# A hybrid transformer's mixing stage: projection jobs placed on both sides of each attention unit's transposes

## The chip, the cores and the metric

The kernel runs on one core of one Trainium2 chip. The metric is the device time of one execution in microseconds; lower is better. TensorE (PE) multiplies, VectorE (DVE) and ScalarE (ACT) work beside it, SyncE (SP) issues the DMAs, and GpSimd (POOL) has nothing to do in the part that is changed. Each engine runs its own instructions in program order, and semaphores join them.

## The reference

The computed function is a one-layer block (retention and RWKV mixing, then a mixture of experts) followed by a two-layer block, for 256 tokens of width 1024, all in float32. The change lies in the two layers of the second block, which are, for each layer:

```python
h = rmsnorm(x, norm_mix[layer])
z = h @ w_in[layer]                       # 18 groups of columns
o_a = nsa_mixer(...)      # compressed, selected and window attention, 4 heads
o_b = diff_mixer(...)     # difference of two softmaxes, 4 heads of 2 halves
o_c = mlstm_mixer(...)    # convolution, gated linear recurrence, 4 heads
o_d = dilated_mixer(...)  # attention over dilated key sets, 4 heads
x = x + concatenate([o_a, o_b, o_c, o_d], axis=-1) @ w_out[layer]
h = rmsnorm(x, norm_ffn[layer])
x = x + (silu(h @ w_gate[layer]) * (h @ w_up[layer])) @ w_down[layer]
```

## The kernel before

`mixing(nc, K, layer)` (L2025) builds one layer's stage from the norm to the product with `w_out`; it is called twice. It holds one instruction stream for each engine: `tensor` (PE), `scalar` (ACT), `vector` (DVE) and `sync` (SP). The order of the work in each is written out by hand in the same lists.

**Jobs.** The projection `h @ w_in` is cut into 22 jobs, `j0` to `j21`. Each is 8 matrix products over the 8 blocks of 128 input features, which the trace shows as 16 matmul records. The jobs `j0`, `j1`, `j14` and `j15` are 512 columns wide (`L2161`), `j20` and `j21` are 256 wide at `L2161`, and the other 16 write 128 feature rows for 256 tokens (`L2158`). ACT copies each result from PSUM to SBUF (`L2342`).

**Other items.** `bq`, `bk`, `aq`, `ks`, `dq` and `dk` are rotations (rotary embedding): one product with a swap matrix on PE (`L2177`, 2 records), then three DVE operations (`rotate`, `L2439`, `L2441`, `L2443`), the last of which counts up `rotated`. `cmp` makes the compressed keys and values (`L2182`, `L2185`), `mq0`, `mq1`, `qk0` and `qk1` belong to the mLSTM, `f` sums its forget gates, and `o0` to `o3` transpose outputs for the last product.

**Banks.** Items take the PSUM banks 6 and 7 in turn (`qk0` and `qk1` take both). PE waits ahead of an item until ACT or DVE has taken the earlier item out of its bank (`held`, `ordinal`).

**Units.** The attention work is 14 units: 0 to 3 are "diff", 4 and 5 "cmp", 6 and 7 "slc", 8 and 9 "win", 10 and 11 "mlstm", 12 and 13 "dil". A unit goes round all three engines:

- `score(u)` on PE (`L2231` for diff, `L2254`, `L2238`) makes the scores in banks 0 and 1, once the scores before have been taken (`scores_kept`).
- `maxima(u)` on DVE (`L2460` masks and moves them, `L2471` takes the row maxima).
- `exps(u)` on ACT (`L2365` and `L2363`).
- `weigh(u)` on DVE (`L2490` to `L2494` for diff, `L2508` for others) normalises and counts up `p_ready`.
- `turn(u)` on PE (`L2268`, `L2264`) transposes the probabilities; it waits for `p_ready`.
- `keep(u)` on ACT (`L2383`, `L2377`) copies them to SBUF.
- `values(u)` on PE (`L2289`, `L2282`) multiplies them with the values, and `output(u)` on DVE takes the result.

**Order on PE.** First the items of `before_units`, then `score(0)`, and then for each unit u: `score(u + 1)`, `turn(u)`, the items of `fills[u]`, `values(u)`. All filling jobs of a unit stand behind its transposes. `score(0)` follows `j7`, which follows `bk`.

**Order on ACT.** The copies of all `before_units`, then the exponentials for `lambdas` and `forget_gates` (`L2407`, `L2409`, with the load of the table for Exp ahead of them), `exps(0)`, and for each unit `keep(u)`, `exps(u + 1)`, the copies of `fills[u]`. Behind those of unit 4 stands a block of other functions (`L2419` to `L2424`), with three table loads.

**Order on DVE.** `lambdas()`, `rotate("bq")`, `rotate("bk")`, `forget_gates()`, a wait for ACT's exponentials (`lam_exp`) with two small operations (`L2595`, `L2596`), `maxima(0)`, and for each unit `weigh(u)`, `maxima(u + 1)`, `output(u - 1)`, then `convolve()` (`L2553`, `L2556`) in unit 0, `cut_blocks()` (`L2569`, behind the copy of `j11`) in unit 1, and the rotations of `fills[u]`.

The weights come as 2 MB slots of a ring of five (`WeightStream`), loaded as PE starts on a later slot. `K.both` shares semaphores between the two layers.

Of the kernel before, what the change touches and what calls it, by code (L numbers as in the profile page):

```python
# [15 lines left out]
KT = D // P  # L16
# [2008 lines left out]
def mixing(nc, K, layer):  # L2025
# [19 lines left out]
    f, fa = A.temp(TT, 4), A.temp(TT, 4)  # L2045
# [26 lines left out]
    before_units = ["j0", "j1", "j2", "j3", "j4", "bq", "j5", "j6", "bk", "j7"]  # L2072
    fills = [["j8", "j9"], ["j10", "j11"], ["j12", "j13", "cmp"], ["aq", "j14"], ["ks", "j15"], ["j16", "mq0"], ["j17", "mq1"],
             ["j18", "f"], ["j19", "dq"], ["j20", "dk", "qk0"], ["j21", "qk1"], ["o0"], [], []]
    after_units = ["o3", "o1", "o2"]
    (x_in, x_at), place_free = K.x_ready, K.place_free
    items = before_units + [name for fill in fills for name in fill] + after_units
    at = {name: n for n, name in enumerate(items)}
    by = lambda name: "dve" if name in turns or name in ("f", "qk0", "qk1") else "act"
    ordinal = [sum(by(other) == by(name) for other in items[:n + 1]) for n, name in enumerate(items)]  # L2080
    banks, held, turn_of = [], [], {6: -1, 7: -1}
# [49 lines left out]
    def tensor(pe):  # L2131
# [13 lines left out]
        def job(n, bank):  # L2145
# [5 lines left out]
            for k in range(KT):  # L2151
# [14 lines left out]

        def item(name):
            n = at[name]
            for m in held[n]:
                pe.wait_ge(took[by(items[m])], ordinal[m])  # L2170
            bank = banks[n][0]
            if name[0] == "j":
                last = job(int(name[1:]), bank)
# [123 lines left out]
        score(0)  # L2297
        for u in range(NU):
            if u + 1 < NU:
                score(u + 1)  # L2300
            turn(u)
            for name in fills[u]:
                item(name)
            values(u)
# [28 lines left out]
    def scalar(act):  # L2333
# [70 lines left out]
        for name in before_units:  # L2404
            item(name)
# [3 lines left out]
        nc.scalar.activation(fa, fa, ACT.Exp, scale=-1.0).then_inc(f_exp, 1)  # L2409
        exps(0)  # L2410
        for u in range(NU):
            keep(u)
            if u + 1 < NU:
                exps(u + 1)
            for name in fills[u]:
                item(name)
# [13 lines left out]
    def vector(dve, meanwhile):  # L2430
# [160 lines left out]
        rotate("bq")  # L2591
        rotate("bk")
# [3 lines left out]
        link(nc.vector.tensor_scalar(nlam, nlam, -lam_init, None, ALU.add))  # L2596
        maxima(0)
        for u in range(NU):
# [5 lines left out]
            if u == 0:  # L2604
                convolve()
            if u == 1:
                cut_blocks()
            for name in fills[u]:
# [661 lines left out]
```

## Time and profile before

| what | us |
|---|---|
| median of 3 runs | 2032.84 |
| lowest and highest of them | 2032.58, 2036.86 |
| the profiled execution's own time | 2041.22 |
| its span in the trace | 2039.3 |
| PE busy (matmuls) | 1699.0 |
| DVE busy | 699.8 |
| ACT busy | 358.4 |

The two mixing stages lie at about 1166 to 1376 us (layer 0) and 1599 to 1810 us (layer 1) of the span; a feed-forward stage follows each. In the timeline a line merges the neighbouring instructions of one source line; the length is from the first start to the last end, and since matmuls are pipelined the next line may start a little before that. The number in brackets is the idle time of the engine just before the line. "PEclk" in the windows is the granted clock of TensorE as a share of its full speed; its two levels are 0.50 (1.2 GHz) and 1.00 (2.4 GHz), and a window in between holds a change.

### The profile page before, as it was taken

The page shows a single profiled execution, that of the slowest core. Times are in us where ns is not written, and L with a number is a line of the kernel's source. Part 1 is how long each engine was busy: PE and PEld are TensorE (multiplying, and loading weights), DVE is VectorE, ACT ScalarE, POOL GpSimd, SP SyncE. Part 2 cuts the span into 40 slices and gives each one's busy share as a digit, 9 for nine tenths or more (in the row PEclk, how much of TensorE's full clock was granted, in tenths as well). Part 3 has the DMA queues.
Part 4 walks back from the last instruction along what each step waited for, and adds up shares of the span by engine and source line. Part 5 has one row for each costly group of instructions (what it writes and reads, how often), then busy time and mean ns, then how long its engine had stood idle before and what let it go on. Part 6 is the DMA issues. An engine that isn't in the chain of part 4 may idle for free.

```text
span 2039.3 us, 31978 instructions
## 1 busy us (share of the span) xinstructions
PE 1699.0 (83%) x14184; PEld 1161.0 (57%) x14184; DVE 699.8 (34%) x1247; ACT 358.4 (18%) x827; POOL 90.9 (4%) x94
## 2 busy tenths in 40 slices
PE   6999889988989675565465589989999989899997
PEld 3665458957975531221121266749994566669963
DVE  2005372353332300000000133554663243546663
ACT  2010212332231210000000222421000124310000
POOL 0000004302311000000000000000000000000000
PEclk9999898977999787877787889989999989899999
DMA  9421110040024599999999932214454522125440
GB/s 372 193 100 67 66 50 36 4 166 2 4 88 153 212 430 427 428 428 428 427 427 428 421 107 83 83 47 182 174 184 161 216 83 83 68 98 191 173 184 21
DMA packets 35593, 382.08 MB, mean 187 GB/s; under 512 B 6977, under 2 KB 10433, under 8 KB 12673
## 3 DMA queue, kind: packets, MB, share of 16 engines
q1 hardware_dynamic: 35458, 380.04, 46.5%
q8 instruction: 113, 1.85, 0.4%
q14 instruction: 22, 0.18, 0.0%
HBM read 378.98 MB, written 1.05 MB: 186 GB/s over the span
## 4 chain that ended last, share of the span: by engine, by line
PE 48%; DMA 11%; DVE 4%; ACT 2%; issue 1%; SPq 0%; DVEq 0%; ACTq 0%
PE psum L2722 14%; PE psum L1873 7%; PE psum L2793 7%; DMA arena<-in_w_moe 6%; PE psum L2158 6%; DMA weight_ring<-in_w_moe 5%; PE psum L2161 3%; PE psum L2313 3%; PE psum L1848 3%; PE psum L2289 1%; PE psum L2268 1%; PE psum L1828 1%; PE psum L2177 1%; ACT arena L2365 0%; PE psum L2254 0%
## 5 line engine op out<-in xcount | busy, mean ns | idle before, releaser
L1873 PE MATMUL psum<-weight_ring,arena 128*32 128x512 f32 x640 | 142.3, 721 | 127.8 <-DMA arena<-in_w_moe 93.7
L1269 PE MATMUL psum<-arena 64*64 64x64 f32 x4608 | 152.4, 224 | 20.5 <-PEq L962 9.1
L2722 PE MATMUL psum<-arena 128*128 128x128 f32 x1408 | 165.2, 275 | 1.7 <-DVE arena L2925 1.7
L2722 PEld LDWEIGHTS psum<-arena 128*128 128x128 f32 x1408 | 161.1, 192 | 2.0 <-issue 2.0
L1269 PEld LDWEIGHTS psum<-arena 64*64 64x64 f32 x4608 | 144.7, 139 | 28.0 <-issue 23.9
L1873 PEld LDWEIGHTS psum<-weight_ring,arena 128*32 128x32 f32 x640 | 35.9, 129 | 205.5 <-issue 205.5
L2002 DVE COPY arena<-psum 128x512 f32<-128x512 f32 x16 | 11.1, 692 | 371.1 <-PE psum L1873 371.1
L2722 PE MATMUL psum<-arena,weight_ring 128*128 128x128 f32 x1056 | 131.9, 283 | 4.7 <-ACT arena L2839 2.7
L1873 PE MATMUL psum<-arena 128*32 128x512 f32 x384 | 106.8, 716 | 33.6 <-DMA weight_ring<-in_w_moe 33.1
L2722 PEld LDWEIGHTS psum<-arena,weight_ring 128*128 128x128 f32 x1056 | 127.3, 199 | 5.9 <-DVE arena L2970 3.1
L2158 PE MATMUL psum<-arena,weight_ring 128*128 128x256 f32 x512 | 123.8, 401 | 0.0
L2158 PEld LDWEIGHTS psum<-arena,weight_ring 128*128 128x128 f32 x512 | 103.0, 204 | 18.7 <-ACT arena L2342 1.8
L2908 DVE TENSOR_TENSOR arena<-weight_ring 128x1024 f32<-128x1024 f32 (+1 forms) x72 | 81.3, 1129 | 55.4 <-PE psum L2793 55.2
L1453 DVE TENSOR_TENSOR arena<-arena,psum 128x512 f32<-128x512 f32 (+1 forms) x80 | 50.6, 633 | 88.1 <-PE psum L1269 87.3
L2793 PE MATMUL psum<-arena 128*128 128x512 f32 x176 | 78.5, 592 | 0.0
L2161 PE MATMUL psum<-weight_ring,arena 128*128 128x512 f32 (+1 forms) x192 | 76.2, 552 | 2.6 <-DVE arena L2582 1.3
L2793 PE MATMUL psum<-weight_ring,arena 128*128 128x512 f32 x132 | 63.3, 620 | 9.7 <-DVE arena L2908 6.0
L434 PE MATMUL psum<-arena,weight_ring 128*128 128x256 f32 x288 | 65.7, 391 | 2.8 <-PEq L198 2.8
L1923 ACT ACTIVATE arena<-psum 128x256 f32<-128x256 f32 x16 | 6.2, 386 | 348.0 <-PE psum L1883 348.0
L434 PEld LDWEIGHTS psum<-arena,weight_ring 128*128 128x128 f32 x288 | 56.4, 197 | 11.4 <-issue 3.3
L1848 PE MATMUL psum<-arena 128*128 128x512 f32 x128 | 59.3, 605 | 1.2 <-ACT arena L1938 1.2
L2313 PE MATMUL psum<-weight_ring,arena 128*128 128x512 f32 x128 | 59.4, 624 | 0.0
(497 smaller groups left out, 2252.4 us busy)
## 6 DMA issues: line engine op xcount, KB each, us to landing
weight_ring<-in_w_moe SPq DMA_DIRECT2D x60, 2048.0 KB, 20.2
arena<-in_w_moe SPq DMA_DIRECT2D x36, 2048.0 KB, 20.5
weight_ring<-in_w_in SPq DMA_DIRECT2D x23, 2048.0 KB, 8.4
weight_ring<-in_w_mod SPq DMA_DIRECT2D x12, 2048.0 KB, 8.1
weight_ring<-in_w_gate SPq DMA_DIRECT2D x12, 2048.0 KB, 7.7
weight_ring<-in_w_up SPq DMA_DIRECT2D x12, 2048.0 KB, 7.6
weight_ring<-in_w_down SPq DMA_DIRECT2D x12, 2048.0 KB, 7.6
weight_ring<-in_w_out SPq DMA_DIRECT2D x6, 2048.0 KB, 7.8
```

The source lines that it names most:

```text
L434: last = nc.tensor.matmul(bank[:, 0:T], w[:, k, P * b:P * b + P], hT[:, k, T:2 * T], start=(k == 0), stop=(k == KT - 1))
L1269: last = nc.tensor.matmul(K.ps[half[d], bank, column + HD * n:column + HD * n + HD], lhs(d, h), rhs(d, h), start=True, stop=True, skip_gro ...
L1453: done = nc.vector.tensor_tensor(inv[:, par, 0:kinds, which, :], inv[:, par, 0:kinds, which, :], src, ALU.add)
L1828: last = nc.tensor.matmul(K.ps[:, d % 4, 0:256], K.h2[:, t, P * d:P * d + P], sel[:, t, cols], start=(t == 0), stop=(t == 1))
L1848: last = nc.tensor.matmul(K.ps[:, 2 * t + n, :], scatter_to[:, e, P * t:P * t + P], parts[:, n, :], start=(e == 0), stop=(e == NE - 1))
L1873: last = nc.tensor.matmul(K.ps[strip(j), 4, :], xsT[:, k, CAP * e:CAP * e + CAP], ws[j][:, k, :], start=(k == 0), stop=(k == KT - 1), skip ...
L2158: last = nc.tensor.matmul(K.ps[:, bank, 0:T], w[:, k, P * b:P * b + P], hT[:, k, :], start=(k == 0), stop=(k == KT - 1))
L2161: last = nc.tensor.matmul(K.ps[:, bank, 0:width], hT[:, k, P * b:P * b + P], w[:, k, 0:width], start=(k == 0), stop=(k == KT - 1))
L2313: last = nc.tensor.matmul(K.ps[:, 2 * t + n, :], K.mixT[:, k, P * t:P * t + P], ws[n][:, k, :], start=(g == 0 and k == 0), stop=(g == 2 an ...
L2722: last = nc.tensor.matmul(K.ps[:, bank, P * n:P * n + P], lhs, rhs, start=(n == 0 and k == 0 and name in ("m1", "m5", "m6")), stop=(k == 3 ...
L2793: return nc.tensor.matmul(K.ps[:, int(name[1]) - 1, :], lhs, rhs, start=(j == 0), stop=(j == NFT // 2 - 1), skip_group_check=True)
L2908: nc.vector.tensor_tensor(out, x, y, op).then_inc(sums_ready, 1)
```

## The change

The orders of the three engines in `mixing` are changed, in both layers. No product, copy or vector operation is added or dropped; seven jobs are issued in two halves of 8 records each.

- `j7` leaves `before_units`. On PE it now stands behind `score(0)`, so `score(0)` follows `bk` at once. On ACT its copy stands behind `exps(0)`.
- For the units 0 to 3 one job (`leads`: `j8`, `j10`, `j12`, `j14`) stands on PE between `score(u + 1)` and `turn(u)`, and its copy on ACT ahead of `keep(u)`. The other items stay behind the transposes.
- For the units 4 to 10 one job (`halved`: `j15` to `j21`) is split: four of its eight blocks ahead of `turn(u)`, four behind. Its copy on ACT stands behind `exps(u + 1)`.
- In unit 3 `aq` is now behind `j14`, and in unit 4 `ks` behind `j15`; before, they stood ahead of these jobs.
- The exponentials of `lam` and the forget gates move on ACT from behind all of `before_units` to behind `j1`.
- On DVE `forget_gates()`, the wait for `lam_exp` and the two operations behind it move ahead of `rotate("bq")`, and `convolve()` moves from unit 0 to unit 3. `cut_blocks()` stays in unit 1.

```diff
--- before.py
+++ after.py
@@ -2069,12 +2069,16 @@
     units = [("diff", t, i) for t in range(TT) for i in range(2)]
     units += [(kind, t, 0) for kind in ("cmp", "slc", "win", "mlstm", "dil") for t in range(TT)]
     NU = len(units)
-    before_units = ["j0", "j1", "j2", "j3", "j4", "bq", "j5", "j6", "bk", "j7"]
-    fills = [["j8", "j9"], ["j10", "j11"], ["j12", "j13", "cmp"], ["aq", "j14"], ["ks", "j15"], ["j16", "mq0"], ["j17", "mq1"],
-             ["j18", "f"], ["j19", "dq"], ["j20", "dk", "qk0"], ["j21", "qk1"], ["o0"], [], []]
+    before_units = ["j0", "j1", "j2", "j3", "j4", "bq", "j5", "j6", "bk"]
+    first_fill = "j7"
+    leads = {0: "j8", 1: "j10", 2: "j12", 3: "j14"}
+    halved = {4: "j15", 5: "j16", 6: "j17", 7: "j18", 8: "j19", 9: "j20", 10: "j21"}
+    fills = [["j9"], ["j11"], ["j13", "cmp"], ["aq"], ["ks"], ["mq0"], ["mq1"], ["f"], ["dq"], ["dk", "qk0"], ["qk1"], ["o0"],
+             [], []]
+    around = lambda u: [leads[u]] if u in leads else [halved[u]] if u in halved else []
     after_units = ["o3", "o1", "o2"]
     (x_in, x_at), place_free = K.x_ready, K.place_free
-    items = before_units + [name for fill in fills for name in fill] + after_units
+    items = before_units + [first_fill] + [name for u, fill in enumerate(fills) for name in around(u) + fill] + after_units
     at = {name: n for n, name in enumerate(items)}
     by = lambda name: "dve" if name in turns or name in ("f", "qk0", "qk1") else "act"
     ordinal = [sum(by(other) == by(name) for other in items[:n + 1]) for n, name in enumerate(items)]
@@ -2142,13 +2146,13 @@
                     last = nc.tensor.transpose(K.ps[:, 4 - 2 * place + q, P * k:P * k + P], h[:, t, c:c + P], K.ident)
                 last.then_inc(t_made, 1)
 
-        def job(n, bank):
+        def job(n, bank, ks):
             s, kind, b, width, dst = jobs[n]
             first = s != slot[0]
             if first:
                 slot[0], slot[1] = s, W.take(pe)
             w = slot[1]
-            for k in range(KT):
+            for k in ks:
                 if n == 0 and k == 4:
                     turn_input(1, 0)
                 if n == 1 and k == 0:
@@ -2164,13 +2168,23 @@
                     last.then_inc(W.used, 1)
             return last
 
+        def await_bank(name):
+            for m in held[at[name]]:
+                pe.wait_ge(took[by(items[m])], ordinal[m])
+
+        def half_job(name, i):
+            if i == 0:
+                await_bank(name)
+            last = job(int(name[1:]), banks[at[name]][0], range(4 * i, 4 * i + 4))
+            if i == 1:
+                last.then_inc(made, 1)
+
         def item(name):
             n = at[name]
-            for m in held[n]:
-                pe.wait_ge(took[by(items[m])], ordinal[m])
+            await_bank(name)
             bank = banks[n][0]
             if name[0] == "j":
-                last = job(int(name[1:]), bank)
+                last = job(int(name[1:]), bank, range(KT))
             elif name in turns:
                 pe.wait_ge(rope_landed, 16 * len(rope_in))
                 kept({"bq": "j3", "bk": "j5", "aq": "j9", "ks": "j13", "dq": "j17", "dk": "j19"}[name])
@@ -2295,10 +2309,17 @@
         for name in before_units:
             item(name)
         score(0)
+        item(first_fill)
         for u in range(NU):
             if u + 1 < NU:
                 score(u + 1)
+            if u in leads:
+                item(leads[u])
+            if u in halved:
+                half_job(halved[u], 0)
             turn(u)
+            if u in halved:
+                half_job(halved[u], 1)
             for name in fills[u]:
                 item(name)
             values(u)
@@ -2401,17 +2422,24 @@
         keep_turned(0, 1)
         norm(1, 0)
         keep_turned(1, 0)
-        for name in before_units:
+        for name in before_units[:2]:
             item(name)
         act.wait_ge(lam_ready, once)
         nc.scalar.activation(lsum, lsum, ACT.Exp).then_inc(lam_exp, 1)
         act.wait_ge(f_abs, once)
         nc.scalar.activation(fa, fa, ACT.Exp, scale=-1.0).then_inc(f_exp, 1)
+        for name in before_units[2:]:
+            item(name)
         exps(0)
+        item(first_fill)
         for u in range(NU):
+            if u in leads:
+                item(leads[u])
             keep(u)
             if u + 1 < NU:
                 exps(u + 1)
+            if u in halved:
+                item(halved[u])
             for name in fills[u]:
                 item(name)
             if u == 4:
@@ -2588,12 +2616,12 @@
         scale_turned(1, 0)
         dve.wait_ge(rest_landed, 16 * len(rest_in))
         lambdas()
-        rotate("bq")
-        rotate("bk")
         forget_gates()
         dve.wait_ge(lam_exp, once)
         link(nc.vector.tensor_tensor(nlam, lsum[:, 1:2], lsum[:, 0:1], ALU.subtract))
         link(nc.vector.tensor_scalar(nlam, nlam, -lam_init, None, ALU.add))
+        rotate("bq")
+        rotate("bk")
         maxima(0)
         for u in range(NU):
             weigh(u)
@@ -2601,10 +2629,10 @@
                 maxima(u + 1)
             if u:
                 output(u - 1)
-            if u == 0:
-                convolve()
             if u == 1:
                 cut_blocks()
+            if u == 3:
+                convolve()
             for name in fills[u]:
                 if name in turns:
                     rotate(name)
```

## Rows read from the trace of the kernel before

**Rows 1.** Head of the page: the span, then busy time by engine.

```profile
span 2039.3 us, 31978 instructions
...
PE 1699.0 (83%) x14184; PEld 1161.0 (57%) x14184; DVE 699.8 (34%) x1247; ACT 358.4 (18%) x827; POOL 90.9 (4%) x94
```

**Rows 2.** Waits of PE, 1638.38 to 1755.32 us: who waited for whom, total, times, longest.

```profile
PE psum L2268 <- DVE arena L2494: 6.8, 2, 3.7
```

**Rows 3.** Timeline of PE, layer 1: start, length, line, tiles, count, [idle before, releaser].

```profile
1599.24 1.09 PE L2142 MATMUL psum<-arena 128*128 128x128 f32 x8 [2.14 <-DVE arena L2578]
...
1637.52 1.02 PE L2177 MATMUL psum<-arena 128*128 128x512 f32 x2
1638.38 3.63 PE L2158 MATMUL psum<-arena,weight_ring 128*128 128x256 f32 x16
1641.94 0.71 PE L2231 MATMUL psum<-arena 32*128 32x128 f32 x8
1645.18 1.18 PE L2231 MATMUL psum<-arena 32*128 32x128 f32 x8 [2.53 <-DVE arena L2460]
1649.49 0.69 PE L2268 MATMUL psum<-arena 128*128 128x128 f32 x2 [3.13 <-DVE arena L2494]
1649.97 9.82 PE L2158 MATMUL psum<-arena,weight_ring 128*128 128x256 f32 x32
...
1661.46 7.10 PE L2158 MATMUL psum<-arena,weight_ring 128*128 128x256 f32 x32
```

**Rows 4.** The same timeline, around the transposes of the third unit.

```profile
1673.69 1.12 PE L2268 MATMUL psum<-arena 128*128 128x128 f32 x4 [3.68 <-DVE arena L2494]
1674.60 9.46 PE L2158 MATMUL psum<-arena,weight_ring 128*128 128x256 f32 x32
```

**Rows 5.** Windows on PE, layer 1: length, busy (instructions), granted clock, DMA.

```profile
1600.00:1602.00 2.00, 0.72 (x5) 0.72 0.97 410
1644.00:1646.00 2.00, 0.82 (x8) 0.82 0.00 0
1654.00:1656.00 2.00, 2.00 (x8) 0.62 0.00 0
1672.00:1674.00 2.00, 0.31 (x2) 0.64 0.00 0
1684.00:1764.00 80.00, 74.55 (x513) 1.00 0.22 80
1768.00:1770.00 2.00, 0.49 (x3) 0.53 0.00 0
1780.00:1782.00 2.00, 2.00 (x4) 0.55 0.71 164
```

**Rows 6.** Timeline of DVE, layer 1, same columns as Rows 3.

```profile
1639.90 0.69 DVE L2443 TENSOR_TENSOR arena<-arena 128x512 f32<-128x512 f32 x1
...
1644.05 0.16 DVE L2595 TENSOR_TENSOR arena<-arena 128x1 f32<-128x1 f32 x1 [2.67 <-ACT arena L2407]
...
1644.43 0.69 DVE L2460 SCALAR_TENSOR_TENSOR arena<-psum,arena 128x512 f32<-128x512 f32 x1
...
1669.08 2.25 DVE L2569 TENSOR_TENSOR arena<-arena 64x240 f32<-64x240 f32 x4 [5.10 <-ACT arena L2342]
```

**Rows 7.** Timeline of PE, layer 1, the later units.

```profile
1714.29 1.10 PE L2282 MATMUL psum<-arena 15*128 15x64 f32 x8
...
1717.54 0.66 PE L2268 MATMUL psum<-arena 128*128 128x128 f32 x4 [1.08 <-DVE arena L2508]
...
1739.49 1.09 PE L2268 MATMUL psum<-arena 128*128 128x128 f32 x8 [0.48 <-DVE arena L2508]
...
1755.32 1.14 PE L2207 MATMUL psum<-arena 64*128 64x256 f32 x8 [1.19 <-ACT arena L2342]
```

**Rows 8.** Timeline of PE, layer 0: the same stretch's first and last lines.

```profile
1205.66 3.63 PE L2158 MATMUL psum<-arena,weight_ring 128*128 128x256 f32 x16
...
1322.03 1.14 PE L2207 MATMUL psum<-arena 64*128 64x256 f32 x8 [1.19 <-ACT arena L2342]
```

## The prediction

> **What bounds the kernel now.** I read the head of the page first [rows 1]: PE has a matmul in flight for 1699 of 2039.3 us, and DVE and ACT are below half of that. A change that adds and drops no operation can then only win where PE stands still or runs at its low clock inside the two changed stages. So the second view was the waits of PE from the start of `j7` to the start of `qk1` [rows 2], which names DVE and ACT as releasers and no DMA. The third was PE's timeline of the same stretch [rows 3, 4, 7], where each wait has its place. The fourth was the granted clock there [rows 5], and the last DVE's timeline [rows 6], to see what holds the releasers up. The stretch takes 116.94 us in layer 1 (1638.38 to 1755.32) and 116.37 us in layer 0 (1205.66 to 1322.03) [rows 3, 7, 8], and the two look alike line for line. So I cost layer 1 and count it twice.
>
> Two places lose most. **At the start of the units** PE goes from `score(0)` to `score(1)` over 2.53 us of idle time and from there to `turn(0)` over 3.13 us [rows 3]. The reader is to see why in [rows 6]: DVE is done with `bk` at 1640.59 (1639.90 and 0.69) but stands for 2.67 us until ACT has worked off `j7`'s copy, a table load and two exponentials, and takes up the scores only at 1644.43. From there the round over maxima, exponentials and `weigh(0)` takes 5.06 us to `turn(0)` at 1649.49, and nothing fills it. **At the third unit** `turn(2)` waits 3.68 us [rows 4]; in the DVE timeline `cut_blocks()` waits for the copy of `j11`, runs 2.25 us, and `weigh(2)` stands behind it [rows 6]. Later there are 1.08 us (`turn(6)`) and 0.48 us (`turn(10)`) [rows 7].
>
> Each of the two big waits also costs clock. The granted clock is 0.82 in the window 1644 to 1646, so it falls to 0.50 there, and is 0.62 in 1654 to 1656, so it is back only then; it falls again within 1672 to 1674 [rows 5]. The two jobs behind the first take 9.82 us where two undisturbed ones take 7.10 (16 records follow each other in 3.47) [rows 3]; those behind the second take 9.46 [rows 4].
>
> **The change part by part.** All for one stage.
>
> *`j7` behind `score(0)`, ACT's exponentials and DVE's small work ahead.* DVE will come from `rotate("bk")` straight to `maxima(0)`. The 2.67 us on DVE goes; its cover is the time ahead of `bq`, in which DVE has nothing to do but wait for PE. The ACT step that moves is a table load and two short exponentials, between the copies of `j1` and `j2`, which lie 3.5 us apart; if that were late, `j4` would wait for its bank, a few tenths. The round of 5.06 us starts about 0.8 us after `score(0)` starts. Between that start and `turn(0)` PE now has `score(0)` and `score(1)` (0.64 us each by the pace of the 0.71 us row) and `j7` and `j8` (3.47 each), 8.2 us against 5.9. So both waits go: 2.53 + 3.13 = 5.66 us. With them goes the low clock: 9.82 - 7.10 = 2.72 us on the jobs, 1.18 - 0.71 = 0.47 on `score(1)` and about 0.2 on `turn(0)`. That is 9.0 us.
>
> *The new wait for `bk`.* What is late next is the rotation itself. `j7` was its cover. From the start of the product of `bk` at 1637.52 to the end of the third DVE operation at 1640.59 are 3.07 us, of which 0.86 are the product's own; with 0.06 us to reach PE `score(0)` waits 2.27 us. Behind it on PE waits everything. Cost 2.27 us.
>
> *A job ahead of `turn(2)`.* The chain from the end of `j11` over its copy, `cut_blocks()` and `weigh(2)` is not shortened, but `j12` (3.47) now lies in the 3.68 us wait. 0.2 us are left. The low clock behind it (9.46 - 7.10 = 2.36 on the jobs, 1.12 against 0.66 us on the transposes, say 0.4) goes too. Gain 3.47 + 2.8 = 6.2 us. `convolve()` moves to unit 3, where `j14` on PE (512 columns, twice the length of a job of 256) covers it; without that cover it would hold up `rotate("aq")` and `weigh(4)` by its own length.
>
> *Halved jobs.* Half a job is 1.73 us or more, above 1.08 and 0.48, so these 1.56 us go. The other half still covers `keep(u)`, about 0.7 to 1.2 us. The halves cost no record more: nothing.
>
> *`ks` behind `j15`.* Before, `j15` hid its rotation. Now only `values(4)` (8 records as in the 1.10 us row, 1.03 by pace) stands between `ks` and `score(6)` [rows 7]. By the same 3.07 us: 3.07 + 0.06 - 0.86 - 1.03 = 1.24 us of new wait. The bounds are 0, if `values(4)` were late itself, and 2.3, if nothing covered it; I take 1.24. `aq` loses its cover too, but has two units until `score(6)`. ACT's copies ahead of `keep(u)` add perhaps 0.1 us in unit 3.
>
> *What stays.* The 1.19 us ahead of `qk1` [rows 7], a like one ahead of `qk0`, and everything behind unit 10: from `qk1` on the order is the old one.
>
> *The clock at the new wait.* The trace has no wait at this place. The nearest row is `L2142` in the same layer: behind 2.14 us of idle time, 1.09 us of work and 1.28 us idle the clock was at 0.72 in the window, thus falling [rows 3, 5]. The waits of 1.19 us and below did not lower it: 1.00 from 1684 to 1764. A wait of 2.27 us with dense work on both sides is between these. If it falls, the price is between 1.4 us (half of the loss behind the first big wait, since no second wait prolongs it) and 2.8 us; if not, nothing. I take one fall in the two stages, 2 us together. The Trainium skill, "TensorE: Matmul & The Clock Gate", Part 1, says that the low clock is the default and that sustained activity releases it; taken strictly, both new waits of each stage could bring it back, and the sum below would lose up to 11 us. The rows agree that idle time of this size can be followed by a fall, and no row shows one behind 1.2 us.
>
> **Sum.** Removed 9.0 + 6.2 + 1.6 = 16.8 us; added 2.3 + 1.2 + 0.1 = 3.6 us; net 13.2 us in a stage, and 26.4 in two. Less 2 for the clock: 24.4. Walking through the stage engine by engine with the same durations, and not by differences, I get 102.9 us for the stretch of 116.94, 14.0 us less, so the differences are a little short. I take **25 us**. The stages behind start with the same queue states as before, and the weight loads are released by PE's own progress, so nothing is known that gives it back. The profiled execution would go from 2041.2 to 2016.2. The runs' median was 8.4 us below that execution; the gain is in microseconds, so the forecast is 2032.8 - 25 = **2007.8**.
>
> What can still move it is the low clock at the end of each stage, 0.53 in 1768 to 1770 and 0.55 in 1780 to 1782, so about 13 us at half speed [rows 5]. It isn't touched by the change, but where it starts may shift with everything ahead, about 2 us either way in a stage.
>
> **The rivals.**
>
> *A. As above*, a gain of 20 to 31 us: 2002 to 2013. Chance 0.74. The range inside it comes from 14.0 us a stage and a luckier end (2 x 14 + 3) down to both stages falling at `bk`.
>
> *B. The clock falls at the new waits and stays low.* Each stage then loses not 1.4 but 4 to 7 us, since low-clock stretches last as long as short products and small waits go on, as the one from 1768 to 1781. Gain 12 to 20 us, some 2017. The same page of the Trainium skill (A second HAM failure mode) tells of a kernel whose engine idles briefly between groups of products so often that the clock keeps changing. For it: the unit loop has five small waits left. Against it: from 1684 to 1764 the loop had such waits and the clock was 1.00 throughout [rows 5]. Chance 0.12.
>
> *C. `turn(2)` is still late.* The change leaves `cut_blocks()` behind `j11` in unit 1, and the cover of 3.47 is below the wait of 3.68. If ACT's copy of `j11` comes late, because the copy of `j10` and `exps(2)` now stand between, the wait grows again and the clock falls with it: the 6.2 us of each stage is lost. Gain 13 us, 2020. Against it: in the walk `exps(2)` ends ahead of `j11`. Chance 0.08.
>
> *D. Slower: the half clock holds through the fills.* Place: from the new wait for `bk` on, where `score(0)` and `score(1)` are products on 32 rows and halves of jobs alternate with transposes. Price: a job of 3.47 us costs that much again. It decides from 13.2 us of work a stage, four jobs; were it held over seven jobs (24 us), each stage would lose 11 us net: 2055. For it: the low stretch of 13 us at the end of the stage. Against it: behind both big waits the clock was back within two jobs [rows 5]. Chance 0.03.
>
> *E. No effect*, because the wait only moves on to ACT, whose block with three table loads now comes behind `j15`'s second half and ahead of `keep(5)`: it would have to cost over 12 us a stage, more than it lasts, and in the walk it ends ahead of `values(5)`. Chance 0.03.
>
> **How the numbers follow.** The forecast is that of A, 2007.8. A with the luckier end reaches down to 2001; C and most of B are inside an upper end of 2018. A measurement of this kernel can tell about 0.2%, 4 us. Faster by more: A, B, C and a little of the others, 0.95; the same 0.03; slower 0.02.
>
> **What would show it.** In the profile after: `score(0)` waits some 2.3 us for `L2443`, and the 2.53 and 3.13 us waits are gone; `turn(2)` waits below 0.5 us; a new wait of about 1.2 us ahead of `score(6)`; no waits at `turn(6)` and `turn(10)`; from `j7` (now behind `score(0)`) to `qk1` with the wait and `score(0)` counted in, 103 to 105 us. I would be wrong if the windows behind `bk` stay at 0.50 for more than two jobs, if `turn(2)` still names DVE with over 1 us, or if the stretch shortens by 13 us and the stages behind take longer.

## The result and the profile after

| | before | changed |
|---|---|---|
| median of the runs, us | 2034.8 (4 runs) | 2014.85 (4 runs) |
| lowest and highest | 2032.58, 2036.86 | 2012.65, 2020.45 |
| profiled execution's span, us | 2039.3 | 2015.2 |

The ratio of the times is 0.9899, with a 95% interval from 0.988 to 0.9918. In a second measurement it was 0.9885 (0.9864 to 0.9906). The change is faster by 20 us, where 25 were forecast and the range held 15 to 32. The time of 2014.85 us is 7 us above the forecast of 2007.8: 5 of them are the smaller gain, and 2 come from the base, since the median of before is 2034.8 with a fourth run and was 2032.84 when the forecast was made.

The head of the page after answers to [rows 1]. PE is busy 8 us less, though it executes the same 14184 matmuls: they ran at the low clock for less time.

```profile
span 2015.2 us, 31978 instructions
...
PE 1690.9 (84%) x14184; PEld 1151.5 (57%) x14184; DVE 700.5 (35%) x1247; ACT 355.9 (18%) x827; POOL 91.0 (5%) x94
```

PE's timeline in layer 1 answers to [rows 3] and [rows 4] (start, length, line, tiles, count, [idle before, releaser]). `L2191` is the product of `bk`, `L2245` scores, `L2162` jobs of 256 and `L2282` transposes.

```profile
1623.53 1.02 PE L2191 MATMUL psum<-arena 128*128 128x512 f32 x2
1626.66 0.71 PE L2245 MATMUL psum<-arena 32*128 32x128 f32 x8 [2.11 <-DVE arena L2471]
1627.30 5.41 PE L2162 MATMUL psum<-arena,weight_ring 128*128 128x256 f32 x16
...
1633.29 3.73 PE L2162 MATMUL psum<-arena,weight_ring 128*128 128x256 f32 x16
...
1654.66 0.66 PE L2282 MATMUL psum<-arena 128*128 128x128 f32 x4
```

The 2.53 and 3.13 us waits are gone, and so is the 3.68 us one: `turn(2)` at 1654.66 has no bracket. In their place `score(0)` waits 2.11 us, and the job behind it, `j7`, takes 5.41 us instead of 3.63. The later units, which answer to [rows 7]:

```profile
1682.45 1.10 PE L2296 MATMUL psum<-arena 15*128 15x64 f32 x8
1684.79 0.72 PE L2268 MATMUL psum<-arena 64*128 64x128 f32 x8 [1.24 <-DVE arena L2471]
1685.44 3.39 PE L2162 MATMUL psum<-arena,weight_ring 128*128 128x256 f32 x8
...
1731.56 1.14 PE L2221 MATMUL psum<-arena 64*128 64x256 f32 x8 [1.18 <-ACT arena L2363]
```

`score(6)` waits 1.24 us for the rotation of `ks`, and half a job behind it takes 3.39 us where half a job takes 1.9 to 2.0. The two waits of 1.08 and 0.48 us have no line any more. The waits view over the stretch from `bk`'s product to `qk1` names all that is left (who waited for whom, total, times, longest), against 6.8 us for one of its groups alone in [rows 2]:

```profile
PE psum L2245 <- DVE arena L2471: 2.1, 1, 2.1
PE psum L2268 <- DVE arena L2471: 1.2, 1, 1.2
PE psum L2221 <- ACT arena L2363: 1.2, 1, 1.2
PE psum L2221 <- DVE arena L2467: 0.9, 1, 0.9
```

DVE's timeline answers to [rows 6]. It goes from the rotation (`L2471`) to the first maxima (`L2488`) in 0.8 us, waiting only for the scores:

```profile
1625.91 0.69 DVE L2471 TENSOR_TENSOR arena<-arena 128x512 f32<-128x512 f32 x1
1627.42 0.69 DVE L2488 SCALAR_TENSOR_TENSOR arena<-psum,arena 128x512 f32<-128x512 f32 x1 [0.82 <-PE psum L2245]
```

The windows of PE (length, busy, granted clock, DMA share, GB/s) answer to [rows 5]. Behind each of the two new waits the clock is at its lower level for one short stretch:

```profile
1626.00:1628.00 2.00, 1.34 (x11) 0.96 0.69 295
1628.00:1630.00 2.00, 2.00 (x7) 0.50 0.00 0
1684.00:1686.00 2.00, 1.21 (x10) 0.97 0.00 0
1686.00:1688.00 2.00, 2.00 (x6) 0.50 0.64 139
```

Layer 0 looks the same. Its stretch, which answers to [rows 8]:

```profile
1201.03 1.02 PE L2191 MATMUL psum<-arena 128*128 128x512 f32 x2
...
1308.97 1.14 PE L2221 MATMUL psum<-arena 64*128 64x256 f32 x8 [1.18 <-ACT arena L2363]
```

From the start of `bk`'s product to the start of `qk1` the changed kernel takes 107.94 us in layer 0 and 108.03 in layer 1 (1201.03 to 1308.97, 1623.53 to 1731.56). Before it took 117.23 and 117.80, by the rows of `bk` (layer 1 at 1637.52, [rows 3]) and `qk1` ([rows 7, 8]). So the two stretches give 9.3 + 9.8 = 19.1 us. Layer 0's start of `bk` before, then the first product of the following stage in both layers, before (`L2734`) and after (`L2762`):

```profile
1204.80 1.02 PE L2177 MATMUL psum<-arena 128*128 128x512 f32 x2
...
1377.64 1.06 PE L2734 MATMUL psum<-arena 128*128 128x128 f32 x8 [2.69 <-DVE arena L2966]
...
1811.04 1.06 PE L2734 MATMUL psum<-arena 128*128 128x128 f32 x8 [2.69 <-DVE arena L2966]
```

```profile
1363.71 1.06 PE L2762 MATMUL psum<-arena 128*128 128x128 f32 x8 [2.69 <-DVE arena L2994]
...
1787.03 1.07 PE L2762 MATMUL psum<-arena 128*128 128x128 f32 x8 [2.69 <-DVE arena L2994]
```

From the start of `bk`'s product to there it is 172.84 and 173.52 us before and 162.68 and 163.50 after, so the two stages give 10.2 + 10.0 = 20.2 us, and the whole gain of 20 us is theirs. The spans differ by 24.1 us; the other 4 are not the change's: layer 0's stage alone starts 3.8 us earlier (1162.64 against 1166.41), in code that is the same in both kernels. The stretch and the stage, not the span, are what the experiments are read by.

### The profile page after: what moved, and what is told of

Its sections match the earlier page's. It is cut to its first block, busy times and chain, and to the rows that moved or that the text cites. A ratio compares the mean times of both kernels' runs of the same rounds, so it can differ in the third digit from the quotient of the medians.

```text
span 2015.2 us, 31978 instructions
## 1 busy us (share of the span) xinstructions
PE 1690.9 (84%) x14184; PEld 1151.5 (57%) x14184; DVE 700.5 (35%) x1247; ACT 355.9 (18%) x827; POOL 91.0 (5%) x94
## 4 chain that ended last, share of the span: by engine, by line
PE 50%; DMA 11%; DVE 3%; ACT 1%; issue 1%; SPq 0%; DVEq 0%; ACTq 0%
PE psum L2750 14%; PE psum L1873 7%; PE psum L2821 7%; DMA arena<-in_w_moe 6%; PE psum L2162 6%; DMA weight_ring<-in_w_moe 5%; PE psum L2165 3%; PE psum L2334 3%; PE psum L1848 3%; PE psum L2303 1%; PE psum L1828 1%; PE psum L2282 1%; PE psum L2268 1%; PE psum L2191 1%; PE psum L1898 0%
## 5 line engine op out<-in xcount | busy, mean ns | idle before, releaser
L2750 PEld LDWEIGHTS psum<-arena,weight_ring 128*128 128x128 f32 x1056 | 127.2, 199 | 5.9 <-DVE arena L2998 3.1
L2162 PE MATMUL psum<-arena,weight_ring 128*128 128x256 f32 x512 | 124.2, 396 | 0.0
L2162 PEld LDWEIGHTS psum<-arena,weight_ring 128*128 128x128 f32 x512 | 98.6, 197 | 19.7 <-issue 4.1
L434 PEld LDWEIGHTS psum<-arena,weight_ring 128*128 128x128 f32 x288 | 56.4, 197 | 11.3 <-issue 3.3
L2334 PE MATMUL psum<-weight_ring,arena 128*128 128x512 f32 x128 | 59.1, 622 | 0.0
## 6 DMA issues: line engine op xcount, KB each, us to landing
weight_ring<-in_w_moe SPq DMA_DIRECT2D x60, 2048.0 KB, 20.2
```

Source lines behind the costliest of these rows:

```text
L434: last = nc.tensor.matmul(bank[:, 0:T], w[:, k, P * b:P * b + P], hT[:, k, T:2 * T], start=(k == 0), stop=(k == KT - 1))
L2162: last = nc.tensor.matmul(K.ps[:, bank, 0:T], w[:, k, P * b:P * b + P], hT[:, k, :], start=(k == 0), stop=(k == KT - 1))
L2334: last = nc.tensor.matmul(K.ps[:, 2 * t + n, :], K.mixT[:, k, P * t:P * t + P], ws[n][:, k, :], start=(g == 0 and k == 0), stop=(g == 2 an ...
L2750: last = nc.tensor.matmul(K.ps[:, bank, P * n:P * n + P], lhs, rhs, start=(n == 0 and k == 0 and name in ("m1", "m5", "m6")), stop=(k == 3 ...
```

## The experiments

Below, "stretch" always means from the start of `bk`'s product to the start of `qk1`, and "stage" from the same start to the first product of the following stage. Two numbers are layer 0 and layer 1.

| kernel | stretches, us | stages, us | median, us | ratio to before (95%) |
|---|---|---|---|---|
| before | 117.23, 117.80 | 172.84, 173.52 | 2034.8 | 1 |
| changed | 107.94, 108.03 | 162.68, 163.50 | 2014.85 | 0.9899 (0.988 to 0.9918) |
| changed, again | 107.93, 108.04 | 162.66, 163.51 | 2016.43 | 0.9885 (0.9864 to 0.9906) |
| e5_early_exps | 114.27, 114.79 | 169.69, 170.29 | 2026.43 | 0.9962 (0.9946 to 0.9979) |
| e8_before_filler | 112.09, 112.09 | 166.80, 167.74 | 2023.74 (one run) | |
| e1_filler | 104.86, 104.86 | 159.58, 160.18 | 2006.41 | 0.9866 (0.9846 to 0.9886) |
| e3_ks_first | 107.82, 107.92 | 162.55, 163.44 | 2015.42 | 0.9906 (0.9887 to 0.9925) |
| e4_whole | 107.91, 109.64 | 162.64, 164.31 | 2014.49 (one run) | |
| e2_covered | 103.06, 104.70 | 158.89, 160.15 | 2008.47 | 0.9873 (0.9852 to 0.9895) |
| e6_moved | 99.76, 99.76 | 159.15, 156.51 | 2007.00 | 0.9859 (0.9842 to 0.9876) |
| e7_later | 96.20, 96.20 | 158.56, 158.03 | 2002.97 | 0.984 (0.9815 to 0.9864) |
| e9_tail_filler | 96.20, 96.20 | 151.44, 151.44 | 1988.20 | 0.9752 (0.9729 to 0.9774) |

The kernels ran on several chips, and the median of before was 2034.8 to 2040.5 us on them; the ratios are the fair comparison of whole times, and intervals that overlap don't separate two kernels.

The question was why two waits of 2.1 and 1.2 us cost more than their own length, and whether the forecast gain went there or somewhere else. The theory was that the clock falls behind each of them. The rivals were that the cutting of jobs costs it, that waits move on to another engine, or that the fall is a matter of chance.

### Holding the clock in the changed kernel: e1_filler

```diff
         for name in before_units:
             item(name)
+        hold_clock(5)
         score(0)
...
             values(u)
+            if u == 4:
+                hold_clock(3)
```

`hold_clock(n)` issues `nc.tensor.matmul(K.ps[:, 2, 0:T], hT[:, 0, 0:P], hT[:, 0, :], start=True, stop=True)` n times.

> Extra work: 10 records of a 256-wide product (2.17 us) into the idle PSUM bank 2 between bk and score(0), 6 records (1.30 us) between values(4) and score(6); the results are never read. Stretch means from the start of bk's product to the start of qk1 (changed kernel 108.0 us in both layers). Theory 'idle time lowers the clock': the two low-clock stretches behind the new waits are gone, the waits become work of the same length, stretch 108.0 - 2 x 1.6 = 104.8 us, total about 6.4 us less than the changed kernel. Rival 'the clock falls because of the short products around the waits (32-row scores, 15-row values), or by chance': stretch 108.0 or a little more, clock still below 1.00 behind both.

PE's timeline of layer 1 around the first of them, `L2308` being the extra products, then the windows over the two stretches:

```profile
1616.98 1.02 PE L2191 MATMUL psum<-arena 128*128 128x512 f32 x2
1617.84 2.32 PE L2308 MATMUL psum<-arena 128*128 128x256 f32 x10
1620.11 0.71 PE L2245 MATMUL psum<-arena 32*128 32x128 f32 x8
1620.75 3.74 PE L2162 MATMUL psum<-arena,weight_ring 128*128 128x256 f32 x16
```

```profile
1616.98:1721.84 104.86, 102.80 (x634) 1.00 0.26 96
1197.92:1302.78 104.86, 102.79 (x633) 1.00 0.26 96
```

The extra products take the place of the wait (1617.84 to 1620.11), `score(0)` starts as late behind `bk` as before, and nothing useful came earlier. Still `j7` (1620.75) takes 3.74 us instead of 5.41, the clock is 1.00 throughout, and each stretch is 3.1 to 3.2 us shorter, as against the 3.2 expected. The two falls of the clock in each stage are thus shown to cost 6.2 us in the two stretches together, and to come from PE standing still, not from the kind of products around the waits.

### The same in the kernel before: e8_before_filler

```diff
             if u == 0:
+                hold_clock(5)
             if u + 1 < NU:
                 score(u + 1)
+            if u in (0, 2):
+                hold_clock({0: 7, 2: 8}[u])
             turn(u)
```

> Kernel before with extra products into the idle PSUM bank 2, whose results are never read, in its three big waits: 10 records (2.17 us) ahead of score(1), 14 (3.04) ahead of turn(0), 16 (3.47) ahead of turn(2). The waits themselves stay. Theory 'a third of what the change gained is clock': the clock stays at 1.00 over the whole stretch and it shortens from 117.8 and 117.2 by 6.2 us to 111.4. Rival 'the gain is the idle time alone': 117 or more.

```profile
1201.07:1313.16 112.09, 107.81 (x658) 1.00 0.25 90
1625.89:1737.98 112.09, 107.81 (x658) 1.00 0.25 90
```

With its three big waits filled by useless products the old order takes 112.09 us in both layers, 5.1 and 5.7 less. So of the 9.3 to 9.8 us that the change gains in a stretch, more than half could be had without moving any useful work. The expected 6.2 us were too much. In layer 1 the difference is the 0.47 us of the slow `score(1)`: `turn(0)` waits for DVE in any case, and starts 7.55 us behind `score(0)` in both kernels. In layer 0 the falls of before cost 0.6 us less than in layer 1.

### Only the small work moved: e5_early_exps

```diff
-        for name in before_units:
+        for name in before_units[:2]:
             item(name)
         act.wait_ge(lam_ready, once)
...
+        for name in before_units[2:]:
+            item(name)
         exps(0)
```

On DVE `forget_gates()`, the wait for `lam_exp` and its two operations stand ahead of `rotate("bq")`, as in the change.

> Kernel before with only the early exponentials on ACT and the early small work on DVE; every job stays where it was. DVE no longer stands 2.67 us between rotate(bk) and maxima(0). Theory: maxima(0) starts 0.2 us behind score(0) instead of 1.9, score(1) waits 0.8 us instead of 2.53, turn(0) still some 3.1 to 3.6 us; stretch (from bk's product to qk1, before 117.8 and 117.2) 1.7 us shorter, more by up to 2.7 only if the clock no longer falls. Rival 'the table load delays the copies of j2 and j3': the wait comes back ahead of bq, no gain.

```profile
1625.52 1.02 PE L2177 MATMUL psum<-arena 128*128 128x512 f32 x2
...
1631.44 0.71 PE L2231 MATMUL psum<-arena 32*128 32x128 f32 x8 [0.80 <-DVE arena L2462]
1635.75 0.69 PE L2268 MATMUL psum<-arena 128*128 128x128 f32 x2 [3.59 <-DVE arena L2496]
```

`score(1)` waits 0.80 us and `turn(0)` 3.59 us, both as worked out. The stretches are 3.0 us shorter in both layers, not 1.7. `turn(0)` starts 5.82 us behind `score(0)`, where it was 7.55: that is the 1.7. The rest is clock, though the clock still falls at both places: the two jobs behind the wait take 8.99 us where they took 9.82, those behind `turn(2)` 9.04 where they took 9.46. The expectation had allowed for a change of the clock's part only if it no longer fell.

### The wait for ks taken away: e3_ks_first

```diff
+    early = {4: "ks"}
-    fills = [..., ["aq"], ["ks"], ["mq0"], ...]
+    fills = [..., ["aq"], [], ["mq0"], ...]
```

`early` puts `ks` on PE ahead of both halves of `j15`, and its rotation on DVE ahead of the items of `fills[4]`.

> Only ks back ahead of j15 (which stays halved); the order at score(0) is the changed kernel's. Theory: the wait of 1.24 us ahead of score(6) and the low clock behind it go, stretch 108.0 - 2.85 = 105.2 us. Rival 'only the idle time counts': 106.8 us; rival 'turn(5) or values(4) takes the wait over': no change.

This missed. The wait of `score(6)` is gone, and the time stayed. PE's timeline, then the line of ACT's for the copy of `j16`, in layer 1:

```profile
1673.86 1.13 PE L2192 MATMUL psum<-arena 128*128 128x512 f32 x2
...
1692.30 3.65 PE L2163 MATMUL psum<-arena,weight_ring 128*128 128x256 f32 x8 [1.07 <-ACT arena L2366]
```

```profile
1691.88 0.36 ACT L2366 ACTIVATE arena<-psum 128x256 f32<-128x256 f32 x1
```

A wait of 1.07 us stands ahead of the first half of `j17` now, with the low clock behind it (3.65 us for half a job). `j17` needs the bank of `j16`, whose copy on ACT (1691.88) stands behind the block of unit 4 with its three table loads, and behind `exps(6)` with a fourth. The rival "another takes the wait over" is right, at a place that no theory had named.

In layer 0 the same wait of 1.07 us brought no fall. There the clock fell 30 us later, behind the wait of 0.86 us ahead of `qk0`, a wait that before and the changed kernel have too, without a fall:

```profile
1297.57 0.71 PE L2222 MATMUL psum<-arena 64*128 64x128 f32 x8 [0.86 <-DVE arena L2470]
...
1300.14 3.54 PE L2253 MATMUL psum<-arena 128*128 128x128 f32 x16
```

`L2253` takes 2.00 us for its 16 records at the full clock, so this fall too cost some 1.6 us, and the two stretches come out alike.

### Whole jobs behind the transposes: e4_whole

```diff
-    halved = {4: "j15", 5: "j16", 6: "j17", 7: "j18", 8: "j19", 9: "j20", 10: "j21"}
+    halved = {}
+    fills = [..., ["j15", "ks"], ["j16", "mq0"], ["j17", "mq1"], ["j18", "f"], ...]
```

> Changed kernel with j15 to j21 no longer halved but whole behind the transposes as before the change (ks stays behind j15). Theory: the waits of 1.08 us at turn(6) and 0.48 at turn(10) come back, seven times the 0.1 us that a job loses by being cut go: stretch 108.0 + 1.56 - 0.7 = 108.9 us. Rival 'cutting is free': 109.6 us. Rival 'the waits do not come back in the new order': 107.3.

```profile
1251.17 0.60 PE L2278 MATMUL psum<-arena 128*16 128x128 f32 x4 [1.17 <-DVE arena L2513]
1251.61 7.03 PE L2165 MATMUL psum<-weight_ring,arena 128*128 128x512 f32 x16
...
1291.49 1.09 PE L2282 MATMUL psum<-arena 128*128 128x128 f32 x8 [0.48 <-DVE arena L2536]
```

Of the two old waits only the one of `turn(10)` (0.48 us, at 1291.49) came back. In place of 1.08 us at `turn(6)` there are 1.17 us at `turn(5)` (`L2278`), since `weigh(5)` on DVE now stands behind the rotation of `ks`. These lines are layer 0's, where the job behind `turn(5)` takes 7.03 us. In layer 1 the wait is 1.18 us, and the clock falls behind it:

```profile
1673.66 0.77 PE L2278 MATMUL psum<-arena 128*16 128x128 f32 x4 [1.18 <-DVE arena L2513]
1674.23 8.60 PE L2165 MATMUL psum<-weight_ring,arena 128*128 128x512 f32 x16
```

So layer 0 has one fall (behind `score(0)`'s wait) and layer 1 has two, and their stretches of 107.91 and 109.64 us differ by 1.7 us, the price of one fall, although the lines of waits are the same. The changed kernel has two falls in each layer. Compared at equal falls, layer 1 against layer 1, halving the jobs is worth 109.64 - 108.03 = 1.6 us a stage. That is the idle time that it covers (1.18 + 0.48 us), so the cutting itself costs next to nothing here, as the rival "cutting is free" had it. The run also shows that a wait of 1.24 us needn't lower the clock: `score(6)` waits that long in both layers (at 1261.77 and 1685.95), and the windows from 1260 to 1268 and from 1678 to 1690 are at 1.00.

### Both waits covered by order alone: e2_covered

```diff
-    before_units = [..., "j6", "bk"]
-    first_fill = "j7"
-    halved = {4: "j15", ...}
+    before_units = [..., "j6", "bk", "j7"]
+    halved = {0: "j9", 4: "j15", ...}
```

`ks` comes first, as in e3_ks_first.

> j7 back between bk and score(0), the unit 0 gets j8 and half of j9 ahead of its transposes and the other half behind; ks back ahead of j15. Both new waits lose their place. Theory 'the two new waits cost their idle time and a low clock each': stretch 108.0 - (2.1 + 1.7) - (1.2 + 1.6) = 101.4 us in both layers, total about 13 us below the changed kernel. Rival 'the waits only move': turn(0) or values(0) waits 1 to 2 us for DVE or ACT and the clock falls there, stretch 104 us or more.

The stretches are 103.06 and 104.70 us, not 101.4. The wait for `bk` is gone, but `score(1)` waits 0.80 us for its banks, and `j17` 1.06 us for `j16`'s copy as in e3_ks_first; behind the latter the clock fell in layer 1 alone, as in e3_ks_first (half a job takes 3.66 us there and 2.00 in layer 0). That makes the difference of 1.64 us between two otherwise equal layers.

### The waits followed to their causes: e6_moved and e7_later

```diff
+    first_fill = "j8"
+    leads = {1: "j10", 2: "j12", 3: "j14", 9: "j20", 10: "j21"}
+    halved = {0: "j9", 4: "j15", 5: "j16", 6: "j17", 7: "j18", 8: "j19"}
+    early = {4: "ks", 9: "dk"}
...
             keep(u)
+            if u == 5:
+                item(halved[u])
             if u + 1 < NU:
                 exps(u + 1)
```

The last part is on ACT, and puts the copy of `j16` ahead of `exps(6)`.

> e2_covered, with j8 between score(0) and score(1), j16's copy on ACT ahead of exps(6), j20 and j21 whole ahead of turn(9) and turn(10), dk ahead of j20. Theory 'each wait left has one cause, a late copy or rotation': the waits of 0.80 (score(1)), 1.07 (j17), about 0.9 (qk0) and 1.19 (qk1) go, stretch 103.1 - 3.9 = 99.2 us where the clock holds, and it now holds in both layers. Rival 'the waits move on': 102 us or more, with new waits ahead of values(9) or turn(11).

```profile
1201.65:1301.41 99.76, 99.17 (x618) 1.00 0.27 101
```

99.76 us in both layers, at a clock of 1.00, 8.2 us below the changed kernel. But the time didn't follow in full: 2007.0 us, and the two stages together are 10.5 us shorter than the changed kernel's, not 16.4. In the later part of the stage the wait ahead of `turn(11)` grew from 1.00 us to 2.09. This is layer 0:

```profile
1306.31 1.09 PE L2283 MATMUL psum<-arena 128*128 128x128 f32 x8 [2.09 <-DVE arena L2538]
```

Behind it the clock fell in layer 0 and stayed low to 1332; in layer 1 it fell only at `turn(13)`, as before, and the stage there is 2.6 us shorter. e7_later puts `j21` there:

```diff
-    leads = {..., 9: "j20", 10: "j21"}
+    leads = {..., 9: "j20"}
+    halved = {..., 8: "j19", 11: "j21"}
...
-            kept({..., "dil": "j21"}[kind])
+            kept({..., "dil": "j21" if t else "j20"}[kind])
```

> e6_moved, with j21 halved round turn(11) instead of whole ahead of turn(10), values(12) waiting for j20 only. Its 3.5 us leave the stretch up to qk1 and fill waits behind it. Theory: stretch 99.2 - 3.5 = 95.7 us, and from qk1 to the start of the last product (before 22.8 us) at most 2.5 us longer, so about 1 us a layer faster than e6_moved. Rival 'units 10 and 11 are bound by the round over DVE and ACT': a new wait ahead of turn(10) or turn(11), no gain.

```profile
1712.30 3.51 PE L2166 MATMUL psum<-weight_ring,arena 128*128 128x256 f32 x8 [2.94 <-DVE arena L2536]
...
1726.69 1.97 PE L2283 MATMUL psum<-arena 128*128 128x128 f32 x8 [2.65 <-DVE arena L2541]
1729.83 3.68 PE L2304 MATMUL psum<-arena 128*128 128x64 f32 x16 [1.18 <-ACT arena L2407]
```

That it is faster than e6_moved is not shown. The stretch is 3.6 us shorter, but the stage is 0.6 us shorter in layer 0 and 1.5 us longer in layer 1, so the expected 1 us a layer didn't come. The median is lower, 2002.97 us against 2007.00, but the intervals of the two ratios overlap, and in the profiles the whole difference lies ahead of layer 0's stage (5.2 us) and between the stages (4.6 us). The rival was right in part: `j21` waits 2.94 us for its bank, which `qk1` holds until DVE has read it. The rows, of layer 1, show what is left at the end of the stage: 2.65 and 1.18 us of waits for DVE and ACT, with products at half speed behind them (3.68 us for 16 records that take 2.00).

### Holding the clock at the end: e9_tail_filler

```diff
+            if u in (11, 13):
+                hold_clock(12)
...
+            if u == 13:
+                pe.wait_ge(scores_kept, NU)
+                hold_clock(4, 0)
             values(u)
...
+        hold_clock(3, 0)
         item("o3")
```

The base is e7_later. `hold_clock(n, bank)` issues `nc.tensor.matmul(K.ps[:, bank, 0:P], K.ident, K.ones, start=True, stop=True)` n times, in bank 2 or 0.

> e7_later with products into idle banks, results never read, in the waits behind qk1: 24 records of a 128-wide product (2.6 us) ahead of j21 and of turn(13), 8 (0.9 us) ahead of values(13), 6 (0.65 us) ahead of o3. No useful work moves. Theory 'the end of the stage loses clock through its waits': the low-clock stretches behind j21's wait (about 4 us long) and from turn(13) to the first output products (about 14 us) go, some 6 us a layer, total 10 to 12 us below e7_later. Rival 'products of 128 columns are too little to hold the clock there, or the other waits (0.7 us each) let it fall anyway': less than 3 us in all, clock 0.50 behind turn(13).

```profile
1711.24 2.94 PE L2309 MATMUL psum<-arena 128*128 128x128 f32 x24
...
1727.12 1.09 PE L2283 MATMUL psum<-arena 128*128 128x128 f32 x8
...
1732.54 10.46 PE L2346 MATMUL psum<-weight_ring,arena 128*128 128x512 f32 x24
```

```profile
1290.00:1345.00 55.00, 53.42 (x304) 1.00 0.22 77
1700.00:1760.00 60.00, 58.43 (x311) 1.00 0.20 71
```

The clock is 1.00 up to the end of both stages. `turn(13)` takes 1.09 us instead of 1.97, and the first 24 records of the last product 10.46 instead of 12.57. From `qk1` to the end of that product layer 1 takes 52.6 us (1708.49 to 1761.04) against 59.1 in e7_later. The two stages together are 13.7 us shorter than e7_later's, where 10 to 12 were expected. The time is 1988.2 us, a ratio of 0.9752 (0.9729 to 0.9774), the fastest of all kernels here. Of the 52 us between its median and that of before, the two stages give 43.5; the rest lies outside them, and its cause was not looked for.

### The changed kernel again: after_again

> The changed kernel unaltered, on the same chip and beside the same runs of before as the next one. If the granted clock falls behind both new waits wherever the phase of the run lies, the stretch from bk's product to qk1 is 108.0 us in both layers again; if the fall was a matter of chance it is 106.4 or 104.8 in one of them. Time 18 to 22 us below before.

107.93 and 108.04 us again. In two executions of the changed kernel, and with an upstream that ended 1.5 us apart, the clock fell behind both waits in both layers. Behind `score(0)`'s wait of 2.11 us it also fell in both layers of e3_ks_first and e4_whole, eight times of eight. Behind `score(6)`'s wait of 1.24 us it fell four times of four here, but not in e4_whole, with another order ahead of it. So a wait of that size leaves it open whether the clock falls, and what decides was not found.

## Why the prediction was right, and where it was off

- **What bounds the stage.** Right. The waits at `score(1)`, `turn(0)` and `turn(2)` are gone, and e5_early_exps shows that the early exponentials alone bring `turn(0)` 1.7 us nearer to `score(0)`, as expected there.
- **The two big stalls with their clock**, 9.0 + 6.2 us. Right in kind. e8_before_filler gives the clock's part alone as 5.1 and 5.7 us, where the sum counted 6.2; 0.5 of the difference is `score(1)`, whose slowness e8_before_filler can't return, and 0.6 is layer 0, which lost less than layer 1. The prediction had costed layer 1 and counted it twice.
- **`turn(2)`.** Right: 0.2 us of wait was forecast. The timeline puts no bracket there, but `turn(2)` starts 3.76 us behind the start of `j12`, where `turn(1)` starts 3.57 us behind that of `j10`.
- **The new wait for `bk`.** 2.27 us forecast, 2.11 measured; from the start of `bk`'s product to `score(0)` it is 3.13 us in both. **The one for `ks`**: 1.24 and 1.24.
- **The clock at the new waits** was the mis-sized term. The sum took one fall in the two stages, 2 us, and held that a wait of 1.2 us doesn't lower the clock, because [rows 5] shows 1.00 over such waits. There were four falls, of 1.6 us each: 6.2 us by e1_filler. That is 4 of the missing 5 us. The step that failed was to read the absence of a fall behind the waits of [rows 7] as a bound: e3_ks_first shows a fall behind 0.86 us in layer 0, and e2_covered one behind 1.06 us in layer 1. The sentence on the Trainium skill's page "TensorE: Matmul & The Clock Gate", Part 1, that the low clock is the default and activity releases it, was nearer to what happened, but the loss that I worked out from it, 11 us, was too high: a fall among dense jobs costs 1.6 us, not the 2.8 behind a second wait.
- **"The halves cost no record more: nothing."** Nearly right. With scores of 32 or 64 rows ahead of it a job takes 3.57 us to the next start instead of 3.47, and the halves of `j17` take 1.84 and 1.83 us. But the halves of `j20`, with 128-row products on both sides, take 1.73 each, and the transposes behind a job are shorter than behind scores. Added up from start to start at full clock, e1_filler against e8_before_filler, the jobs on `L2162` and the 512-column ones take 1.1 us more a stretch (53.5 against 52.4) and the 128-column transposes 0.4 us less, so 0.7 in all. The walk through the stage gave 102.9 us from the end of `bk`'s product, or 103.8 from its start; e1_filler, with the clock held, took 104.86. These 0.7 us are part of the 1.1 between; the rest was not traced.
- **The sum.** With the clock held the change gains 12.4 and 12.9 us a stretch (117.23 and 117.80 less 104.86), where the sum without the clock said 13.2 and the walk 14.0. Against the sum's 24.4 the two stretches gave 19.1: 4.2 of the 5.3 us are the clock, 1.1 are these differences.
- **The rivals.** B, the clock at the new waits, is what happened, but each fall was as short as A had it. The gain of 20 us is at the lower edge of A, and the time of 2014.85 is 2 us above A's 2002 to 2013, by the base that had moved. C did not happen: `turn(2)` has no bracket. D did not: the job after `j7` takes 3.73 us, the full clock. E, that a wait moves to ACT behind its block of table loads, did not happen in the change, but it did in e3_ks_first, where PE came there without the wait of 1.24 us.

What stays open: why one layer keeps its clock behind the same wait at which the other loses it, and what moves the start of the stages by some us from one profile to the next.

## What to carry to other kernels

Cost a wait of TensorE as its own length plus the work behind it that will run at half clock, and count that as possible for waits of 1 to 2 us too, even amid dense work: here some of them lowered the clock and some did not. When a wait can't be covered by useful work, a few products into an idle PSUM bank return the second part: here that gave 6 us on the changed kernel (its two stretches) and some 13 us at the ends of the two stages of e7_later. Judge an order by the whole stage, not by the part that was worked on: e7_later's stretch was 3.6 us shorter and its stages no shorter. After an order has been improved, read the waits view again to the end of the stage, since here removing one wait brought up the next, as in e3_ks_first and e6_moved.

## What the runs showed of the hardware

- The granted clock fell behind a wait of PE of 2.11 us eight times of eight (two profiles of the changed kernel, e3_ks_first, e4_whole). Behind 1.24 us it fell four times of four in the changed kernel and not in e4_whole's two layers; behind 1.17 to 1.18 us in one of e4_whole's two layers; behind 1.06 to 1.07 us in layer 1 but not in layer 0 of e2_covered and e3_ks_first; behind 0.86 us in layer 0 of e3_ks_first alone. Behind the wait of 1.18 to 1.19 us ahead of `qk1` it fell in none of the nine profiles that have it. One fall amid dense jobs cost 1.6 to 1.7 us. I had expected none behind waits of 1.2 us.
- Products with useless results hold the clock as well as useful ones: 10 and 6 records of 256 columns, or 24, 8 and 6 records of 128, were enough for 1.00 over the filled parts of e1_filler and e9_tail_filler.
- A job of 16 records of 256 columns took 3.47 us to the next start between products of 128 rows, and 3.57 behind score products of 32 rows.
- The profiled spans of kernels with the same code ahead of layer 0's stage place its start up to 8.7 us apart (1157.70 in e5_early_exps, 1166.41 in before), and the times of one kernel scatter over 4 to 16 us. Where that comes from was not tried.
